# Routing expert outputs back to their tokens: row stores and indirect fetches in place of a TensorE scatter

## The reference, cut to what matters

```python
logits = h @ router
top_v, top_i = lax.top_k(logits, 2)
gates = softmax(top_v)
for e in range(8):
    gate_e = sum(where(top_i == e, gates, 0))
    out = out + gate_e * ((silu(h @ wg[e]) * (h @ wu[e])) @ wd[e])   # wg, wu 1024 x 2816, wd 2816 x 1024
y = rmsnorm(x + out)
```

## Time and profile before

| | |
|---|---|
| median of 3 runs | 1323.06 us (1319.23 to 1323.9) |
| profiled execution, its own time | 1327.41 us |
| its span, first to last instruction | 1325.7 us |
| TensorE matmul busy | 1299.6 us, 98% |
| VectorE, ScalarE, GpSimd busy | 373.8, 169.9, 61.0 us |
| moved by DMA | 380.81 MB, mean 287 GB/s |
| transfers of the expert weights | q1, 69.9% of 16 engines over the span |

### The profile page before, as it was taken

One profiled execution on the slowest core, in us unless ns is written; L12 is line 12 of the kernel. 1 busy time (PEld: TensorE's weight loads), 2 busy tenths in 40 slices (PEclk: granted clock), 3 DMA queues, 4 the chain that ended last, 5 costly groups with the idle time before them and its releaser, 6 DMA issues.

```text
span 1325.7 us, 17071 instructions
## 1 busy us (share of the span) xinstructions
PE 1299.6 (98%) x7217; PEld 826.4 (62%) x7217; DVE 373.8 (28%) x869; ACT 169.9 (13%) x367; POOL 61.0 (5%) x87
## 2 busy tenths in 40 slices
PE   8999999999999999999999999999999999999997
PEld 6878788888888888867843433434334444444452
DVE  5537775421111113984400110011100110110101
ACT  2241423010000100013200000000000000101002
POOL 1013110000000201100000000000000000000000
PEclk8999999999999999999799999999999999999999
DMA  8639633565456424354699999999999999899994
GB/s 289 206 130 304 221 96 96 191 179 168 127 166 223 143 72 127 132 198 197 267 388 424 408 424 425 408 424 410 424 425 424 424 406 425 323 359 418 409 423 188
DMA packets 105484, 380.81 MB, mean 287 GB/s; under 512 B 7580, under 2 KB 62796, under 8 KB 80778
## 3 DMA queue, kind: packets, MB, share of 16 engines
q1 hardware_dynamic: 97811, 359.46, 69.9%
q0 software_dynamic: 3216, 11.54, 2.7%
q10 hardware_dynamic: 4386, 8.76, 2.1%
HBM read 371.96 MB, written 8.86 MB: 287 GB/s over the span
## 4 chain that ended last, share of the span: by engine, by line
PE 89%; DVE 7%; ACT 1%; DMA 1%; SPq 1%; issue 1%; DVEq 0%; ACTq 0%
PE ps L1746 30%; PE ps L2278 21%; PE ps L2317 13%; PE ps L2264 6%; PE ps L2272 3%; DVE both L1450 3%; PE ps L1999 3%; PE ps L2328 2%; PE ps L2299 1%; PE ps L1991 1%; PE ps L1977 1%; PE ps L2211 1%; PE ps L2148 1%; PE ps L2200 1%; DMA both<-in_w_in_even_dram 1%
## 5 line engine op out<-in xcount | busy, mean ns | idle before, releaser
L1746 PE MATMUL ps<-both 128*128 128x264 f32 x2080 | 474.3, 390 | 0.5 <-DMA both<-in_w_in_even_dram 0.3
L1746 PEld LDWEIGHTS ps<-both 128*128 128x128 f32 x2080 | 397.0, 192 | 72.3 <-issue 2.7
L2278 PE MATMUL ps<-both 128*64 128x384 f32 (+1 forms) x1792 | 280.9, 466 | 0.8 <-ACT both L1050 0.8
L2278 PEld LDWEIGHTS ps<-both 128*64 128x64 f32 x1792 | 127.0, 138 | 152.6 <-issue 142.7
L2317 PE MATMUL ps<-both 128*64 128x512 f32 (+1 forms) x704 | 176.1, 596 | 0.0
L2317 PEld LDWEIGHTS ps<-both 128*64 128x64 f32 (+1 forms) x704 | 58.5, 143 | 98.6 <-issue 97.8
L1653 DVE TENSOR_TENSOR both<-both,ps 128x384 f32<-128x384 f32 (+7 forms) x46 | 20.9, 485 | 233.2 <-PE ps L2278 118.1
L2264 PE MATMUL ps<-both 128*128 128x510 f32 (+1 forms) x192 | 77.2, 559 | 0.0
L2264 PEld LDWEIGHTS ps<-both 128*128 128x128 f32 x192 | 35.9, 189 | 39.8 <-issue 32.5
L1450 DVE SCALAR_TENSOR_TENSOR both<-both,par 128x256 f32<-128x256 f32 x120 | 50.9, 481 | 1.0
L2272 PE MATMUL ps<-both 128*32 128x384 f32 (+1 forms) x512 | 47.1, 465 | 0.0
(11 more groups left out here) (369 smaller groups left out, 882.4 us busy)
## 6 DMA issues: line engine op xcount, KB each, us to landing
both<-in_moe_w_gate_dram SPq DMA_DIRECT2D x64, 1408.0 KB
both<-in_moe_w_up_dram SPq DMA_DIRECT2D x64, 1408.0 KB
both<-in_moe_w_down_dram SPq DMA_DIRECT2D x48, 1536.0 KB
both<-in_w_in_even_dram SPq DMA_DIRECT2D x10, 2048.0 KB
both<-in_moe_w_down_dram SPq DMA_DIRECT2D x16, 1024.0 KB
both<-in_ffn_w_gate_dram SPq DMA_DIRECT2D x11, 1024.0 KB
both<-in_ffn_w_up_dram SPq DMA_DIRECT2D x11, 1024.0 KB
both<-in_ffn_w_down_dram SPq DMA_DIRECT2D x4, 2816.0 KB
```

The source lines that it names most:

```text
L1746: ins = mm(ps[:, 0:T], w[:, c, cols:cols + P], src[:, c, :], start=c == 0, stop=c == nk - 1)
L2278: ins = mm(ps[64 * r:64 * r + 64, 0:WIDE[k]], xg[:, c, 0:64], w[:, first:first + WIDE[k]], start=c == 0, stop=c == DC - 1)
```

## The change

Each token's outputs take another way back.

- Items 0 to 5 (s < KEPT = 6): ScalarE's queue stores ysb to rows of yrows, a new DRAM tensor with row 0 zero: two stores of 64 rows of 512 values for a 64 item, four for a 96 item (two of 64 and two of 32 rows), one of 128 rows of 1024 for the 128 item. In a 96 item, ScalarE and VectorE first add the two halves of the rows 64 to 95. The next item's ysb copies wait for the stores (y_put).
- After item 0 VectorE works out for each token the one or two rows of yrows that are its own, or row 0, and their gates (`results_chosen`, fourteen small operations).
- In item 5's place on its queue, GpSimd waits for all six puts, then fetches one row for each token (three indirect DMAs of 128, 128 and 8 rows of 4 KB into yback); behind item 6's row fetch come three more for the second rows (`fetch_results`). VectorE multiplies them by the gates and adds them to sums (`results_added`), the first set in item 6 ahead of its products, the second at the end of item 6.
- In items 0, 1 and 2, behind chunk 3, TensorE turns a block of accT back to rows (`turn_sums`, eight transposes), and ScalarE and VectorE copy it to sums.
- Items 6 and 7 build SelG, turn it behind up chunk 1, and scatter right behind their own down products, into six banks, which VectorE adds to sums, one 128 x 512 addition for a bank (`banks_read`). The next item's first chunks wait for the banks; in item 7 the norm reads sums in place of the banks.
- The scatter matmuls of the items 1 to 7, scattered, mark_sums, sum_rows, SelX, and the turns of SelG in the items 1 to 5 are gone. `row_ids` keeps the row numbers. SyncE's piece 11 waits for four stores, the zero row among them. Sixteen small memsets on GpSimd are added and one iota removed; some semaphores elsewhere are merged under one name.

The diff, cut to its core:

```diff
-SCAT = DC // 2
+KEPT = STATIC - 1
...
+ROW_BASE = [1 + sum(SEQ_CAP[:s]) for s in range(KEPT)]
+YROWS = 1 + sum(SEQ_CAP[:KEPT])
+PUTS = {64: 2, 96: 4, P: 1}
+PUT_BASE = [16 * sum(PUTS[SEQ_CAP[k]] for k in range(min(s, KEPT))) for s in range(EXP)]
+LO_BASE = [sum(3 if SEQ_CAP[k] == 96 else 1 for k in range(s)) for s in range(EXP)]
...
-        LAST_BANK = ((1, 3), (0, 2), (7, 5))
...
+        sums = [[reg(19136, 512), reg(19648, 512)], [reg(1536, 512), reg(2048, 512)], [reg(2560, 512), reg(14976, 512)]]
+        yback = [reg(8704 + D * k, D) for k in range(BLK)]
...
+        yrows = nc.dram_tensor("yrows", [YROWS, D], F32).ap()
...
-                        sp.wait_ge(sem("hrows_stored"), 48)
+                        sp.wait_ge(sem("hrows_stored"), 64)
...
+            def fetch_results(m, k):
+
+                n, at = ROWS[k], 1 + BLK * m + k
+                if m:
+                    pool.wait_ge(sem("y_added"), k + 1)
+                pool.indirect_dma_start(
+                    out=yback[k][0:n, :], out_offset=None, in_=yrows[:, :],
+                    in_offset=bass.IndirectOffsetOnAxis(ap=rowidx[0:n, at:at + 1], axis=0)).then_inc(sem("y_back"), 16)
+
...
             for s in range(STATIC):
                 fetch_rows(s, 0)
-            pool.wait_ge(sem("ord_ready"), 2)
+                if s < KEPT - 1:
+                    continue
+                if s == KEPT - 1:
+                    pool.wait_ge(sem("y_chosen"), 1)
+                    pool.wait_ge(sem("y_put"), PUT_BASE[KEPT])
+                for k in range(BLK):
+                    fetch_results(s - KEPT + 1, k)
...
+            act.dma_start(yrows[0:1, :], htok[64:65, 2, :]).then_inc(sem("hrows_stored"), 16)
...
+                if s:
+                    act.wait_ge(sem("y_put"), PUT_BASE[s])
                 a.activation(ysb[0:n, 0:512], psum[6][0:n, :], ACT.Copy).then_inc(sem("ysb_lo"), 1)
+                if cap == 96:
+                    for h in range(2):
+                        a.activation(ysb[64 * h:64 * h + 32, 512:1024], psum[7][64 * h + 32:64 * h + 64, :],
+                                     ACT.Copy).then_inc(sem("ysb_lo"), 1)
+                if s < KEPT:
+                    act.wait_ge(sem("ysb_lo"), LO_BASE[s + 1])
+                    act.wait_ge(sem("ysb_hi"), s + 1)
+                    first = ROW_BASE[s]
+                    if cap == P:
+                        act.dma_start(yrows[first:first + P, :], ysb[:, :]).then_inc(sem("y_put"), 16)
+                    else:
+                        for h in range(2):
+                            act.dma_start(yrows[first:first + 64, 512 * h:512 * h + 512],
+                                          ysb[64 * h:64 * h + 64, 0:512]).then_inc(sem("y_put"), 16)
+                            if cap == 96:
+                                act.dma_start(yrows[first + 64:first + 96, 512 * h:512 * h + 512],
+                                              ysb[64 * h:64 * h + 32, 512:1024]).then_inc(sem("y_put"), 16)
...
-                    act.wait_ge(sem("psum_full"), len(TILES) + 2 * k + h + 1)
-                    a.activation(fsq[0:n, 512 * h:512 * (h + 1)], psum[LAST_BANK[k][h]][0:n, :], ACT.Square,
+                    act.wait_ge(sem("banks_read"), items * 6 + (2 * k + h + 1))
+                    a.activation(fsq[0:n, 512 * h:512 * (h + 1)], sums[k][h][0:n, :], ACT.Square,
...
-            def scattered(n4, n5):
-
-                for b in range(SCAT):
-                    lo, hi = accT[:, b, :], accT[:, SCAT + b, :]
-                    dve.wait_ge(sem("t_full4"), n4 + (b + 1))
-                    v.tensor_tensor(lo, lo, psum[4][:, 0:T], ALU.add).then_inc(sem("t_free4"), 1)
-                    dve.wait_ge(sem("t_full5"), n5 + (b + 1))
-                    v.tensor_tensor(hi, hi, psum[5][:, 0:T], ALU.add).then_inc(sem("t_free5"), 1)
+
+            def results_chosen():
+
+                own, row, gv, first, rest = (rsel[:, k, :] for k in range(5))
...
+                v.tensor_copy(rowidx[:, 1:1 + 2 * BLK], ysel).then_inc(sem("y_chosen"), 1)
+
+            def results_added(m):
+
+                dve.wait_ge(sem("t_free4"), USES[BLK - 1]["res"][0] + 1)
+                dve.wait_ge(sem("t_free5"), USES[BLK - 1]["res"][1] + 1)
+                dve.wait_ge(sem("y_back"), 48 * (m + 1))
+                for k in range(BLK):
+                    rows = ROWS[k]
+                    for h in range(2):
+                        to = sums[k][h][0:rows, :]
+                        v.scalar_tensor_tensor(out=to, in0=yback[k][0:rows, 512 * h:512 * h + 512],
+                                               scalar=gsel[0:rows, 3 * m + k:3 * m + k + 1], in1=to, op0=ALU.mult,
+                                               op1=ALU.add).then_inc(sem("y_added" if h else "sums_added"), 1)
...
-                if s:
-                    scattered(t * STEP4 + USES[s]["scat"][0], t * STEP5 + USES[s]["scat"][1])
...
+                if s >= KEPT:
+                    gates_turned(t * STEP4 + USES[s]["gates"][0])
+                if s == KEPT:
+                    results_added(0)
...
+                if s:
+                    dve.wait_ge(sem("y_put"), PUT_BASE[s])
...
+                if s == KEPT:
+                    dve.wait_ge(sem("y_added"), BLK)
+                    dve.wait_ge(sem("sums_added"), BLK)
+                if s >= KEPT:
+                    if s == STATIC:
+                        dve.wait_ge(sem("banks_read"), t * 6 + 6)
+                    for k in range(BLK):
+                        n = ROWS[k]
+                        for h in range(2):
+                            dve.wait_ge(sem("psum_full"), t * 6 + (len(TILES) + 6 * (s - KEPT) + 2 * k + h + 1))
+                            to = sums[k][h][0:n, :]
+                            v.tensor_tensor(to, to, psum[LAST_BANK[k][h]][0:n, :], ALU.add).then_inc(
+                                sem("banks_read"), 1)
+                if s == KEPT:
+                    dve.wait_ge(sem("banks_read"), 6)
+                    results_added(1)
+                    dve.wait_ge(sem("y_added"), 2 * BLK)
+                    dve.wait_ge(sem("sums_added"), 2 * BLK)
...
+            def turn_sums(k, n4, n5):
 
                 n = ROWS[k]
...
+                for h, count in enumerate((n4, n5)):
+                    pe.wait_ge(sem(f"t_free{4 + h}"), count)
+                    for j in range(4):
+                        ins = tr(psum[4 + h][0:n, P * j:P * (j + 1)], accT[:, 4 * h + j, P * k:P * k + n], ident[:, :])
+                    ins.then_inc(sem(f"t_full{4 + h}"), 1)
 
...
+                    if s and (UP_BANKS if up else GATE_BANKS)[cap][at] in (6, 7) and (cap == 64 or not up):
+                        pe.wait_ge(sem("ysb_lo"), t + LO_BASE[s])
+                        pe.wait_ge(sem("ysb_hi"), t + s)
+                    if s == STATIC and (not up or at < 2):
+                        pe.wait_ge(sem("banks_read"), t * 6 + (5 + at if up else 1 + at))
+                    if up and (cap != 64 or at >= 2):
...
-                if s == STATIC:
-                    mark_sums(False)
                 for c in range(DC):
                     chunk(0, c)
                     if c == 1:
-                        n5 = USES[s]["selT"][1]
-                        turn_gates(t + s, t * STEP4 + USES[s]["selT"][0], None if n5 is None else t * STEP5 + n5,
-                                   (SEQ_CAP[min(s + 1, EXP - 1)], s, t + (s + 2)))
-                    if s and 2 <= c < 2 + SCAT:
-                        scatter(SEQ_CAP[s - 1], t + s, t * STEP4 + USES[s]["selT"][0], t * STEP4 + USES[s]["scat"][0],
-                                t * STEP5 + USES[s]["scat"][1], (c - 2,))
+                        row_ids(SEQ_CAP[min(s + 1, EXP - 1)], t + (s + 2), t * STEP4 + USES[s]["ids"][0])
+                    if c == 3 and s < BLK:
+                        turn_sums(s, *USES[s]["res"])
                 for c in range(DC):
                     chunk(1, c)
...
+                    if s >= KEPT and c == 1:
+                        turn_gates(t + (s - KEPT + 1), t * STEP4 + USES[s]["gates"][0])
...
-                    if s == STATIC and k == 1:
-                        down(k, lambda r: sum_rows(2, 0) if r == 0 else None)
-                    elif s == STATIC and k == 2:
-                        down(k, lambda r: sum_rows(1, 0) if r == 0 else None)
-                    elif s == STATIC and k == 3:
-                        down(k, lambda r: sum_rows(0, 0) if r == 0 else None)
-                    else:
-                        down(k)
+                    down(k)
                     for n in late[k] if k < 2 else ():
                         turn_act(n)
+                if s >= KEPT:
+                    pe.wait_ge(sem("t_free5"), t * STEP5 + (USES[s]["gather"][1] + 1))
+                    pe.wait_ge(sem("t_free4"), t * STEP4 + (USES[s]["gates"][0] + 1))
+                    pe.wait_ge(sem("ysb_lo"), t + (LO_BASE[s] + 1))
+                    pe.wait_ge(sem("ysb_hi"), t + (s + 1))
```

(11 more changed lines are left out.)

233 lines of the change are left out of this document (96 added, 137 removed).

## The result

The kernel after takes 1326.33 us (median of 20 runs, 1323.03 to 1329.37), the kernel before in the same series 1322.66 us (20 runs). The ratio is 1.0029, 95% interval 1.0020 to 1.0039: **3.8 us slower**. I had said 1322.6 us and no change. The value lies in my range, the sign does not lie in my sum of -0.4 us.

What follows compares the result with a forecast made beforehand. TensorE was taken to set the pace by some 5 us, with transfers near their 425 GB/s ceiling. -3.2 + 2.8 = -0.4 us took 1327.41 to 1327.0, thus 1322.6 us for the median; range 1316 to 1331.

Steps and rivals of the forecast that it cites:

- my sum of -0.4 us: Whole kernel: last group of down products 3.2 us earlier, end after it 2.8 us longer, together -0.4 us.
- The ceiling: Weight transfers: the 16 engines together move at most 425 GB/s; above 430 would prove the prediction wrong.
- Rival B: Expert stage: transfers had room, so TensorE's 31.7 us come through less 2.8, giving 1294.2 us; chance 0.12.
- the lead of the transfers: Expert stage: weights land ahead of TensorE's use by 5.8 us at item 5 and 5.3 at the end.
- The idle time: Full ring in item 5: 11.3 us of idle transfer time, all but 0.8 given back (bounds 0 and 3).
- The side traffic: Puts and fetches beside the weights, items 0 to 7: 5.0 + 1.0 + 1.2 + 5.2, 12.4 us in all.
- The bound of 8.2 us for four items: Puts of items 0 to 3: upper bound if half-tile stores cost like half-tile fetches; 5.0 was taken.
- Rival A: Side traffic is dear: puts priced like half-tile fetches, result fetches at 2.2 us; 9.0 more, 1331.6 us; chance 0.22.
- TensorE's saving: Expert stage: net 31.7 us less work on TensorE alone, mostly 27.2 us from the previous item's scatter.
- The tail: After the last down product: scatter 0.6 us earlier, six VectorE additions 3.4 later, +2.8 us; 2.2 with adds at 0.6.
- Rival C: Item 7: TensorE idles up to 30%, its clock falls to 1.2 GHz level, +7 us, 1329.6; chance 0.05.
- Rival D: Item 6: VectorE's wait for the first fetch of results bites, each us past 40 costing a us; chance 0.03.

Runs made afterwards that it cites:

- second profile of before: The unchanged kernel before, profiled a second time; it entered the expert stage at 651.24 us and took 1321.22 us.
- Experiment 5: Kernel after, but TensorE brings the sums into the banks in item 7, without VectorE's six last additions: ratio 1.0021 to before, 1.1 us faster than after.
- experiments 7: Kernel after with idle matmuls added in seven chunks of item 5, making it longer: ratio 1.0065 to before, 4.8 us slower than after.
- 8: Kernel after with gate and up products 1 to 6 of item 5 cut from 510 to 425 columns: ratio 0.9992 to before, 4.9 us faster than after.
- 12: Kernel after with each of the six fetches of results cut to a plain load of 8 rows: ratio 1.0003 to before, 3.4 us faster than after.
- experiment 11: Kernel after with puts cut to one row, fetches of results made plain loads of the same size: ratio 0.9996 to before, 4.4 us faster than after.
- experiment 3: Kernel after with puts cut to one row and fetches of results replaced by 8-row loads: ratio 0.9982 to before, 6.2 us faster than after.
- experiment 9: Kernel after with 128-partition row fetches and TensorE bringing the sums into the banks where it waits: ratio 0.9995 to before, 4.5 us faster than after.

## Why the prediction was wrong

**The ceiling: right.** No long stretch passed 425 GB/s; short ones of 4 to 10 us read up to 443 (1172 to 1176 in the kernel after), over the 430 that I had named as a sign of being wrong, in a view that counts a packet where it starts. Rival B fell with it: 13.6 us of TensorE work went behind item 5 and the stretch kept its length.

**The step that failed is the lead of the transfers**, "2.5 MB or 5.8 us before its use" at the start of item 5 and "the lead is 1310.35 - 1305 = 5.3 us" at the end, which I let the change spend. Two things were wrong with it.

First, a part of this lead cannot be spent. I counted from the bytes to TensorE's start. In the second profile of before the same count gives, at 1044.90: 101.9 MB from there to the last group, 0.8 of them row fetches, of 103.8 that three items need, so 2.7 MB in, less 1.44 for the first piece: 1.3 MB or 3 us, at a moment when TensorE stands waiting for that piece. At the end of the kernel after the same drop of the rate that I took as landing lies at 1302 (188, then 66 GB/s), and TensorE, waiting, starts at 1303.51. So 1.5 us by the one count and 3 by the other read as no lead at all. The Trainium skill (DMA: Bandwidth & Descriptors, Anatomy of one DMA — SWDGE (gpsimd) path) says, of a transfer that GpSimd issues, that most of its fixed cost of about 2 us lies between the last byte and the semaphore; the weight pieces here are issued by SyncE, and the two counts for them lie on either side of that figure. I had let the lead go down to 0.2 us.

Second, the rest of it belonged to that one run. It entered the stage at 658.1, behind 17 us at a granted clock of 0.50, the 1.2 GHz level, in which the transfers went on. They ran ahead by a part of the time that TensorE had lost, 5.8 - 3.0 = 2.8 us at item 5; in the run that entered at 651.24 nothing of it was left by item 3. The run of after has 3.4 us at 0.52 just ahead of its stage (640.30), some 1.6 us lost, and so a little of such a lead too. Experiment 5 is the kernel after up to item 5 and had no such fall ahead of its stage: 1047.99 - 651.91 = 396.1 us, where after and experiments 7, 8 and 12, all with a fall of that kind, have 394.0 to 394.7. So against the second profile of before, which had none either, the way to item 5 is 2.4 us longer by experiment 5 and 1.0 by the run of after; the puts' bytes alone are 3.1.

So up to item 5 I had -5.8 + 5.0 = -0.8 us and it was +1.0; from item 5 to the last group I had -2.4 and it was 0.0.

**The idle time: the second failed step.** "The full ring is 12 pieces or 40.7 us, so it now hardly fills. Of the 11.3 us idle I give back all but 0.8." Measured: 11.5 us idle before, 6.0 after, so 5.5 came back and not 10.5, and 1120 to 1170, which I wanted above 400 GB/s, runs at 373. The rows of the kernel after show where the ring is full:

```profile
1128.88 16.24 SPq L627 DMA_DIRECT2D both<-in_moe_w_gate_dram  x4
...
1134.30 27.47 PE ps L2380 x64
```

```profile
1140.00:1170.00 30.00, 30.00 (x111) 14.39 (x111) 2.19 (x8) 0.60 (x1) 0.00 (x0) 1.00 0.94 342
1170.00:1180.00 10.00, 10.00 (x71) 7.53 (x68) 0.00 (x0) 0.47 (x1) 3.68 (x4) 1.00 1.02 431
```

Nearly all of the idle time, 30 x (1 - 342/425) = 5.9 us, lies between 1140 and 1170. TensorE is then in the down products of item 5, and SyncE can issue a piece only every 5.3 us, as they free the ring, where a piece takes 3.4 us to move (1.44 MB at 425 GB/s). I take the mistake to be the unit. 12 pieces are 40.7 us of transfer time, but as a lead over TensorE they last as long as TensorE takes for them: 12 chunks of 2.4 us of item 6 are 29 us, an estimate from its chunk times. Item 5 earns 33.5 us, more than that, so a surplus of some 4.5 us is lost at its end. Experiments 7 and 8 show in both directions that what TensorE takes longer or shorter in item 5 goes into the idle time; the 29 us themselves no run singles out. In the landing of the last piece this error (5.0 us too early) stands against the lead that was not there at item 5 (5.8 us too late): from item 5's start to the landing I had 5.8 - 10.5 + 7.4 = +2.7 us, and it went from 1300 - 1044.9 = 255.1 to 1302 - 1044.3 = 257.7, +2.6. What remained wrong in this part is the lead at the end: 1304.14 - 1300 = 4.1 us went down to 1.5, a gain of 2.6, where I had 5.3 going down to 0.2.

**The side traffic: right in kind, somewhat too dear.** I had 12.4 us with all fetches and puts. The puts cost their bytes and no more: 4.4 us for all six (experiment 11, good to 2.3) against 5.0 + 1.0 + 1.2. The bound of 8.2 us for four items, which the rule on half-tile transfers (the Trainium skill, SBUF — State Buffer, Door 1: The DMA port swizzle) would have given, did not occur for stores; for fetches into 64 partitions the trace agrees with the rule once more, 348 against 427 GB/s. Rival A is refuted: it ends on the right side, by a mechanism that the runs exclude. In experiment 3 a part of the saved bytes went into idle time.

**TensorE's saving: somewhat too high.** The busy time of the page is 1263.6 us against 1290.8 in the second profile of before, 27.2 less where I had 31.7. Most of it turned into waits: 14.4 us up to item 5 and 14.5 behind it, against 2.6 and 0.9.

**The tail: right.** +2.8 predicted, +2.5 measured with additions of 0.61 instead of 0.7 us; I had given 2.2 for 0.6. The profile of experiment 9 is without it again.

**Rival C** did not occur in the profiled run of the kernel after: item 7 is granted 1.00 with TensorE busy 63.57 of 77.20 us. It did occur in item 7 of two of its variants, experiments 5 and 12, for 3.4 and 3.6 us each (last section), so its chance was not nothing; the price there is 1.7 us and not 7. **Rival D** did not occur: the first fetch of results was issued 12.1 us into item 6 (at 1173.80; I had the put landed after 8), and the six landed 13.8 us after issue in the median, longer than the row fetches' 8.9, but the end of item 6 still came when TensorE had done with it (63.71 busy of 64.60).

Together: +1.8 us up to item 5, +2.4 from there to the last group, -0.3 in the tail, 3.9 us in all, from -0.4 to +3.5. That the value fell into my range was owed to the range's width: the two failed steps partly cancel up to the landing of the last piece, and I had no reason to count on that.

**What the change would have needed.** TensorE's time is worth something only behind the start of item 5, and only until the lead at the end is spent, 2.6 us. The side traffic falls in part on the stretch in which the transfers already set the pace, and the tail is added at full price. No version of the change that computes everything is faster than the kernel before by more than its interval.

## What to carry to other kernels

When one engine is shown busy all the time and the transfers run at their ceiling too, ask for each stretch which of them would wait if the other were faster, and take the lead from a run that shows a wait, not from bytes alone: the distance at which a wait appears is the zero. A ring of buffers, by the count above, is a lead of so many pieces times what the consumer takes for the pieces next in it; behind a long item followed by short ones it is full before the bytes say so (here 5.9 us of idle time where the bytes said 0.8). Work that is taken from the busy engine and paid for in bytes of a saturated queue is a loss wherever the queue leads the pace.
